# First block, norms of a two-block float32 model: GpSimd makes w_lo behind each norm, the first token half goes alone, part of the side products lies between the transposes

## What is computed

```python
def rmsnorm(x, g):
    xf = x.astype(jnp.float32)
    y = xf * lax.rsqrt(jnp.mean(xf * xf, axis=-1, keepdims=True) + EPS)
    return (y * g.astype(jnp.float32)).astype(x.dtype)

for i in range(2):
    h = rmsnorm(x, norm1_g[i])
    z = h @ w_in[i] + b_in[i]
    merged = mlstm_and_retention(z)
    x = x + merged @ w_out[i]
    h2 = rmsnorm(x, norm2_g[i])
    x = x + jnp.square(jax.nn.relu(h2 @ w_ff1[i] + b_ff1[i])) @ w_ff2[i] + b_ff2[i]
    h3 = rmsnorm(x, norm3_g[i])
    x = x + jax.nn.sigmoid(h3 @ w_pe_gate[i]) * (p[i] @ w_pe[i])
x = rmsnorm(x, final_g)
```

## Time and profile before

| | |
|---|---|
| time, median of 3 runs | 3228.33 us (3226.37 to 3233.46) |
| span of the profiled execution | 3219.8 us, 8.5 under that median |
| TensorE busy | 3150.0 us, 98% |
| VectorE | 2121.0 us, 66% |
| ScalarE | 1500.2 us, 47% |
| GpSimd | 485.0 us, 15% |
| first block | to about 1281 us |
| mean granted TensorE clock | 0.992 of full speed |

### The profile page before, as it was taken

One profiled execution on the slowest core, in us unless ns is written; L12 is line 12 of the kernel. 1 busy time (PEld: TensorE's weight loads), 2 busy tenths in 40 slices (PEclk: granted clock), 3 DMA queues, 4 the chain that ended last, 5 costly groups with the idle time before them and its releaser, 6 DMA issues.

```text
span 3219.8 us, 49381 instructions
## 1 busy us (share of the span) xinstructions
PE 3150.0 (98%) x20586; PEld 2790.3 (87%) x20586; DVE 2121.0 (66%) x3125; ACT 1500.2 (47%) x1717; POOL 485.0 (15%) x276
## 2 busy tenths in 40 slices
PE   8999999999999999989999999999999999999998
PEld 8797889797978897878999989888769999999887
DVE  6775665577767655676967755555688767655555
ACT  6444454564444544613444444444445444444443
POOL 0000000000000000000866600000004766200000
PEclk9999999999999999999999999999999999999999
DMA  6454645444546454404554465555524544565553
GB/s 231 154 198 162 222 171 196 171 146 169 198 161 215 181 196 152 179 2 155 183 178 152 148 257 200 190 191 195 183 79 171 181 162 144 220 223 188 193 195 131
DMA packets 87944, 565.12 MB, mean 176 GB/s; under 512 B 10224, under 2 KB 10240, under 8 KB 23856
## 3 DMA queue, kind: packets, MB, share of 16 engines
q1 hardware_dynamic: 80784, 534.81, 46.3%
q0 software_dynamic: 6944, 27.21, 2.5%
HBM read 552.54 MB, written 9.44 MB: 175 GB/s over the span
## 4 chain that ended last, share of the span: by engine, by line
PE 54%; DVE 4%; ACT 1%; issue 0%; DVEq 0%; ACTq 0%
PE bank L2150 22%; PE bank L2177 7%; PE bank L2181 7%; PE bank L2176 7%; PE bank L2131 4%; PE bank L2115 0%; DVE w_lo L2613 0%; PE bank L1845 0%; ACT w_hi L2330 0%; PE bank L1842 0%; PE bank L1841 0%; PE bank L1813 0%; PE bank L1808 0%; PE bank L1809 0%; PE bank L1830 0%
## 5 line engine op out<-in xcount | busy, mean ns | idle before, releaser
L2613 DVE TENSOR_TENSOR w_lo<-raw,w_hi 128x2048 fp32r<-128x2048 f32 x224 | 514.8, 2299 | 344.3 <-ACT w_hi L2330 343.4
L2330 ACT ACTIVATE w_hi<-raw 128x2048 fp32r<-128x2048 f32 x291 | 555.7, 1910 | 335.3 <-PE bank L2150 264.8
L1057 DVE TENSOR_TENSOR w_lo<-raw,w_hi 128x2048 fp32r<-128x2048 f32 x200 | 458.1, 2292 | 314.8 <-ACT w_hi L818 313.1
L818 ACT ACTIVATE w_hi<-raw 128x2048 fp32r<-128x2048 f32 x201 | 384.9, 1917 | 438.9 <-PE bank L548 237.3
L2150 PE MATMUL bank<-act_hi,w_hi 128*128 128x256 f32 x2048 | 489.6, 282 | 0.0
L2150 PE MATMUL bank<-act_lo,w_hi 128*128 128x256 f32 x2048 | 485.0, 280 | 0.0
L2150 PEld LDWEIGHTS bank<-act_hi,w_hi 128*128 128x128 f32 x2048 | 385.9, 188 | 0.2
L2150 PEld LDWEIGHTS bank<-act_lo,w_hi 128*128 128x128 f32 x2048 | 386.0, 188 | 0.0
L2176 PE MATMUL bank<-w_hi,c_hi 128*128 128x512 f32 x992 | 385.9, 389 | 0.0
L2177 PE MATMUL bank<-w_hi,c_lo 128*128 128x512 f32 x992 | 385.9, 389 | 0.0
L1697 POOL TENSOR_TENSOR w_lo<-raw,w_hi 128x2048 fp32r<-128x2048 f32 x68 | 313.5, 4615 | 168.2 <-ACT w_hi L2330 168.0
(11 more groups left out here) (562 smaller groups left out, 5287.0 us busy)
## 6 DMA issues: line engine op xcount, KB each, us to landing
raw<-weights SPq DMA_DIRECT2D x492, 1024.0 KB, 4.8
row<-rows POOLq DMA_DIRECT2D x48, 256.0 KB, 4.3
spill<-staged SPq DMA_DIRECT2D x32, 256.0 KB, 2.8
hid<-spill SPq DMA_DIRECT2D x32, 256.0 KB, 5.0
y<-w_pe POOLq DMA_DIRECT2D x2, 1024.0 KB, 5.0
ln_row_mix<-ln_rows POOLq DMA_DIRECT2D x4, 512.0 KB, 5.3
hid<-keys POOLq DMA_DIRECT2D x2, 1024.0 KB, 6.3
ln_row_ffn<-ln_rows POOLq DMA_DIRECT2D x4, 512.0 KB, 7.8
```

What stands on the lines that cost most here:

```text
L818: nc.scalar.activation(w_hi[:, k % SPLIT, :], raw[:, k % RAW, :], ACT.Copy).then_inc(hi_ready, 1)
L1057: nc.vector.tensor_tensor(w_lo[:, k % SPLIT, :], raw[:, k % RAW, :], w_hi[:, k % SPLIT, :].bitcast(F32), ALU.subtract).then_inc(lo_ready, 1)
L2330: A.activation(hi_of(k), raw[:, k % RAW, :], ACT.Copy).then_inc(hi_ready, 1)
L2613: V.tensor_tensor(lo_of(k), raw[:, k % RAW, :], hi_of(k).bitcast(F32), ALU.subtract).then_inc(lo_ready, 1)
```

## The change

1. GpSimd makes w_lo of three tiles of a layer in place of VectorE: the first of ffa1, the first of peg, and in layer 1 the first of the layer. In its program they stand behind the row loads (the last one ahead of them). It waits for w_hi of the tile and for w_lo of the tile before; VectorE waits for GpSimd's before it makes the next (split_after).
2. VectorE's norm takes a token half at a time: sum, reciprocal, multiply of the first, and only then the sum of the second. The multiply is in two halves of 512 features, and the transposes wait for each apart.
3. ScalarE's squares of the front features stand a tile or more earlier: ahead of w_hi of ffa1's first tile, and ahead of w_hi of the third tile of `ffb2`, 1.
4. The side products of features 0 to 511 lie between the transposes of the token halves: of the first token half in norm 1, of the second in norm 2, into bank 0, whence ScalarE copies them to `pe_sb`. The peg stage keeps the other half.
5. warm ahead of norms 1 and 2 is gone; two memsets move behind norm 0's multiplications.

```diff
@@ table of the semaphores' steps per layer @@
-           "lnf_ready": 1, "m_ready": 1, "merged_ready": 2, "mmask_ready": 4, "pe_mm": 1, "read_act": 16, "read_dve": 28,
+           "lnf_ready": 1, "m_ready": 1, "merged_ready": 2, "mmask_ready": 4, "pe_mm": 3, "pe_held": 2, "read_act": 16, "read_dve": 28,
...
+    pe_sb = y[:, :, :].rearrange("p t n -> p (t n)")[:, 2 * D + 2 * S:2 * D + 2 * S + TT * CW].rearrange("p (t n) -> p t n", t=TT)
@@ GpSimd @@
+            def split_lo(k):
+
+                pool.wait_ge(hi_ready, k + 1)
+                pool.wait_ge(lo_ready, k)
+                nc.gpsimd.tensor_tensor(w_lo[:, k % SPLIT, :], raw[:, k % RAW, :], w_hi[:, k % SPLIT, :].bitcast(F32), ALU.subtract).then_inc(lo_ready, 1)
...
+                else:
+                    split_lo(layer * TILES_A)
                 for r in range(ROWS_A):
...
+                for name in ("ffa1", "peg"):
+                    split_lo(layer * TILES_A + TILE[name, 0])
@@ TensorE @@
                 def normed(i):
                     for t in range(TT):
-                        pe.wait_ge(xn_ready, TT * i + t + 1 + layer * A_LAYER["xn_ready"])
+                        if i and t:
+                            side_product(i - 1)
                         for k in range(KD):
+                            if k % KB == 0:
+                                pe.wait_ge(xn_ready, 2 * (TT * i + t) + k // KB + 1 + layer * A_LAYER["xn_ready"])
...
+                def side_product(n):
+
+                    if n == 0:
+                        pe.wait_ge(pe_loaded, layer * 32 + 32)
+                    wait_read(pe, CHUNK[("out", "ffb2")[n], 0], layer)
+                    for k in range(2):
+                        last = nc.tensor.matmul(psum[0][:, :], pt_sb[:, k, n * P:(n + 1) * P], wpe_sb[:, k, 0:CW], start=k == 0, stop=k == 1)
+                    last.then_inc(pe_mm, 1)
+
+                def side_held(n):
+
+                    pe.wait_ge(pe_held, n + 1 + layer * A_LAYER["pe_held"])
...
-                warm(4, 1)
                 normed(1)
+                side_held(0)
...
-                warm(4, 2)
                 normed(2)
+                side_held(1)
                 nat("peg", 0, act_hi, act_lo, Normed(2))
 
-                pe.wait_ge(pe_loaded, layer * 32 + 32)
-                for i in range(2):
-                    for t in range(TT):
-                        for k in range(2):
-                            last = nc.tensor.matmul(psum[4 + 2 * i + t][:, :], pt_sb[:, k, t * P:(t + 1) * P],
-                                                    wpe_sb[:, k, i * CW:(i + 1) * CW], start=k == 0, stop=k == 1)
+                for t in range(TT):
+                    for k in range(2):
+                        last = nc.tensor.matmul(psum[6 + t][:, :], pt_sb[:, k, t * P:(t + 1) * P], wpe_sb[:, k, CW:D], start=k == 0, stop=k == 1)
@@ ScalarE @@
-            def mean_square(n):
+            def fronts(n):
 
                 front_squares(n)
                 do(nc.scalar.activation(spare[:, :], eps, ACT.Sqrt))
+
+            def rests(n):
+
                 for t in range(TT):
...
+                    if i == 0 and layer == 0:
+                        fronts(0)
                     if i or layer == 0:
-                        mean_square(3 * layer + i)
+                        rests(3 * layer + i)
+                    if i:
+                        act.wait_ge(pe_mm, i + layer * A_LAYER["pe_mm"])
+                        do(nc.scalar.activation(pe_sb[:, i - 1, :], psum[0][:, :], ACT.Copy), pe_held)
...
                 stream("out", 0)
+                fronts(3 * layer + 1)
                 stream("out", 1, left=1)
                 norm(1)
...
                     for i in range(2):
+                        if half and i:
+                            fronts(3 * layer + 2)
                         stream(two, i, left=1 if half and i else 0)
                 norm(2)
@@ VectorE @@
+            def split_after(k):
+
+                dve.wait_ge(lo_ready, k + 1)
+                split_lo(0, k + 1)
...
-                    if i:
-                        dve.wait_ge(half_done, i + layer * A_LAYER["half_done"])
-                        add(name, 1, 0, half_added)
-                        if i == 2:
-                            split_lo(base, TILE["peg", 0])
-                        taken(name, 1)
-                        add(name, 1, 1, half_added)
-                        do.done(read_dve)
                     for t in range(TT):
+                        if i and t == 0:
+                            dve.wait_ge(half_done, i + layer * A_LAYER["half_done"])
+                            add(name, 1, 0, half_added)
+                        elif i:
+                            taken(name, 1)
+                            add(name, 1, 1, half_added)
+                            do.done(read_dve)
                         dve.wait_ge(std_ready, TT * i + t + 1 + layer * A_LAYER["std_ready"])
                         do(V.reciprocal(rstd[:, t:t + 1], rstd[:, t:t + 1]))
-                        do(V.tensor_scalar(gate[:, t, :], x[:, t, :], rstd[:, t:t + 1], None, ALU.mult), xn_ready)
+                        for cs in (slice(0, CW), slice(CW, D)):
+                            do(V.tensor_scalar(gate[:, t, cs], x[:, t, cs], rstd[:, t:t + 1], None, ALU.mult), xn_ready)
                     if i == 0:
+                        do(V.memset(shifted[:, :, 0:3], 0.0))
+                        do(V.memset(val_m[:, :, :, MDV:MDV + 1], 1.0))
+                    if i == 0 and layer == 0:
                         split_lo(base, 0)
...
-                stream("out", 1, left=1)
                 norm(1, "out")
-                split_lo(base, TILE["ffa1", 0] + 1)
+                split_after(base + TILE["ffa1", 0])
...
-                    dve.wait_ge(pe_mm, 1 + layer * A_LAYER["pe_mm"])
+                    if i == 0:
+                        dve.wait_ge(pe_held, 2 + layer * A_LAYER["pe_held"])
+                    else:
+                        dve.wait_ge(pe_mm, 3 + layer * A_LAYER["pe_mm"])
...
-                        do(V.tensor_tensor(pre[:, t, :], psum[4 + 2 * i + t][:, :], gate[:, t, cs], ALU.mult))
+                        do(V.tensor_tensor(pre[:, t, :], psum[6 + t][:, :] if i else pe_sb[:, t, :], gate[:, t, cs], ALU.mult))
```

9 lines of the change are left out of this document (4 added, 5 removed).

## The result

| | before | after | ratio, 95% interval |
|---|---|---|---|
| first comparison | 3224.15 us, median of 20 runs | 3231.91 us, median of 20 runs (3224.57 to 3241.02) | 1.0022 (1.0013 to 1.0032) |
| second comparison | 3222.8 us, median of 23 | 3232.9 us, median of 12 (3226.82 to 3241.23) | 1.0033 (1.0021 to 1.0046) |

By the ratios the changed kernel is slower by 7.1 us (4.2 to 10.3) in the first and 10.6 us (6.8 to 14.8) in the second: the direction that was forecast, at half to three quarters of the 14.2 us. (The medians themselves differ by 7.8 and 10.1.) The time, 3232, lies in the range, near its foot of 3231. The forecast had been added to 3228.33, the median of the first three runs of the kernel before; its median over 20 runs was 4.2 lower, and that alone would put the forecast at 3238.4.

The account below looks back on a forecast made before the run. TensorE, busy 98% of the span, was taken as the bound, idle at the norms. Terms summed to +9.1 us at full clock, plus 5.1 for the clock: +14.2 on 3228.33, 3242.5 us; range 3231 to 3248.5 plus 2.5 of scatter.

Parts of the forecast that it names:

- side products out of peg: Peg stage: eight of the 16 side-product rows leave it, saving 3.5 us per layer, 7.0 for two layers.
- norm 1, full clock: Norm 1: the second token half's transposes start at 437.1 where they started at 431.83, +5.3 us per layer, +10.6.
- norm 2, full clock: Norm 2: transposes at 613.1 against 611.26, +1.9 us per layer, +3.8.
- norm 0 of layer 1, full clock, once: Norm 0 of layer 1: x<-x,pre waits for GpSimd's w_lo, giving back 2.4 us, less 0.4 returned: +2.0, once.
- the hold: Norms: VectorE's multiply waits until GpSimd's running w_lo ends, half-multiplies taking about 3.7 us at norm 1, 2.1 at norm 2.
- the rival with the free multiply: Norms: the multiply runs unhindered beside GpSimd; norm 1 +2.1 us per layer, sum -3.1, 3225.2 us; chance 0.16.
- the cover works as written: Norm 1: front squares end early, GpSimd holds nothing, norm 1 costs nothing; 3220.8 us, 0.23% faster; chance 0.05.
- No warm-up matmuls: Norms 1, 2 and layer 1's norm 0: idle TensorE drops to the lower clock, costing +3.6, +0.8 and +0.7 us.
- the full-clock sum: Whole kernel: all terms without clock loss, -7.0 + 10.6 + 3.8 + 2.0 - 0.3 = +9.1 us.
- held with clock loss: Norms: the multiply is held by GpSimd and the clock drops too, +14.2 us, 3242.5; chance 0.55.
- The rival with the clock staying up: Norms: the multiply is held by GpSimd but full clock stays, +9.1 us, 3237.4; chance 0.22.
- Slower by over 0.2%: Whole kernel: sign of the forecast, chance 0.77, against 0.17 for within 0.2% and 0.06 for faster.

## Why the prediction was right or wrong

Per layer the terms can be set beside what the runs showed, at full clock first:

| term | predicted | measured | from |
|---|---|---|---|
| side products out of peg | -3.5 | -3.3 | stages |
| norm 1, full clock | +5.3 | +5.2 | more warm-up matmuls |
| norm 2, full clock | +1.9 | +2.2 | stages |
| norm 0 of layer 1, full clock, once | +2.0 | +2.1 | first profile |
| start, once | -0.3 | -0.3 to -0.4 | first transposes |
| clock at norm 1 | +1.8 | +1.4 | 6.6 less 5.2 |
| clock at norm 2 | +0.4 | 0 | full clock there in four profiles |
| clock at norm 0 of layer 1, once | +0.7 | 0 to +0.6 | four profiles |
| clock at the start and the gates, once | not there | -5.9 | means of four and four profiles |

**What bounds it, and the hold.** GpSimd's w_lo was put at 429.1 to 433.7 and ran, in a trace 1.7 earlier, from 427.31 to 431.80; the half-multiply was to end 0.3 behind it and did. It took 3.62 us at norm 1 and 2.13 at norm 2; 3.7 and 2.1 were forecast. The row it rested on, a uint32 operation held in the second block, was the right one to take. The rule of the Trainium skill that was cited (SBUF — State Buffer, Who interferes with whom) holds for the fp32 tensor_scalar, and the trace agrees at all four norms 1 and 2: up to 3619 ns against 487.

**The split of norm 1.** Of the 5.2 at full clock, the run with VectorE's w_lo gives 2.2 to ScalarE's order and the sum, where the rival with the free multiply had 2.1; the pair of runs with the sum in either place gives 1.75 to the sum, the run with the sum alone 1.9 at the second half's transposes. The rest, 3.0, is the hold.

**The rival "the cover works as written"** decides, as it said, at the start of GpSimd's w_lo: with ScalarE's old order and the sums in front, the multiply starts 0.1 before GpSimd ends, isn't held, and norm 1 costs 0.0. It was rightly held improbable for this change.

**What failed** is the step under "No warm-up matmuls": the clock fell behind norm 1's long wait, as it said, but the size was wrong, +5.1 in the sum where the places it named gave +3.2 (2 x 1.4, and 0.4 at norm 0). It was too dear at norm 1 (+1.8 for 1.4) and at norm 2 (+0.4 for 0: idle 1.57 and no lower clock in any profile of the changed kernel). It rests on one row, the idle 2.13 at 344.70 with the lower clock behind it, and took that row for a rule. Two other profiles of the kernel before have the same idle stretch at that place and full clock behind it. The changed kernel waits 3.19 us at norm 0 of layer 1 and had full clock behind it once and the lower one three times; with VectorE's w_lo it waits 1.92 at norm 1 and had the lower clock in layer 1 and not in layer 0. Only the 5.05 us of norm 1 had the lower clock behind them every time. Below that the length of the idle stretch alone doesn't decide it in these traces.

The same step left out a term without giving a reason. The kernel before already has stretches at the lower clock, 10.2 and 3.4 us behind layer 1's gates and 6.8 at the start, and the prediction took them as fixed; they differ between profiles of one kernel by up to 6.5 us of time. In the profiles they gave back 5.9 us in the mean: the full-clock sum, +10.0 (+9.1 was forecast), with +3.2 and -5.9 gives +7.3, beside the +7.2 that the traces show at the end of the first block.

That does not explain the timed difference, though the first of the two, +7.1, looks like it. In the timed runs of the second comparison the changed kernel lost 3.1 us more to the clock than the kernel before, which is the +3.2 of the norms with nothing given back. It leaves 7.5 of the 10.6 for the rest, where the stages say 10.0; the interval, 6.8 to 14.8, covers both. (For the first comparison no clock of the kernel before is on record.) Of the 14.2 that were forecast, 1.9 are thus the clock's wrong size at the norms. Why the timed differences are a further 2 to 5 us lower stays open; the interval of the second still covers what is left, that of the first doesn't.

So the likeliest case of the prediction, held with clock loss, happened. The rival with the clock staying up, +9.1, came nearer to both times, but its condition didn't hold: the clock fell at norm 1 in every profile of the changed kernel.

**The range** reached down to 3231 because the case at full clock had to be in it, and the measured 3231.9 is only just inside. 4.2 us of its distance from the forecast come from the base, a median of three runs that lay above that of twenty, and are no part of the reasoning. Slower by over 0.2%, the case with most of the chance, is what both comparisons give, 1.0022 just above that bound, with an interval that reaches below it, and 1.0033 above it with all of its interval.
